# Delta-rule stage of a two-block transformer kernel: heads one by one, and heads in interlocked pairs

## The chip, the cores and the metric

The kernel runs on one core of a Trainium2 chip. The metric is the time on the device in microseconds (us), from the program's start to its end; the number that counts is the median of several executions. One more execution is taken with the hardware profiler; all rows below are from it.

The engines are TensorE (PE; the loading of its weights is shown as PEld), VectorE (DVE), ScalarE (ACT), GpSimd (POOL) and SyncE (SP, which only issues DMAs here). Each runs its own queue in order and waits on semaphores.

## The reference

The whole is a stack of layers on 512 tokens of width 1024: a gated delta rule with attention to a memory of 256 tokens, a gated feed-forward layer, a convolution module, more feed-forward layers and a sparse attention. Only the delta rule changes. For each of 8 heads, with q, k, v from a projection, a causal convolution of four taps and silu:

```python
q = l2norm(q) * GDN_DK ** -0.5
k = l2norm(k)
beta = jax.nn.sigmoid(b)
G = jnp.cumsum(gc, axis=-1)                 # gates
lower = jnp.where(strict, bc[..., :, None] * kk * decay, 0.0)
sol = lax.linalg.triangular_solve(lower + jnp.eye(CHUNK, dtype=f32), rhs, ...)
...
def step(state, xs):                        # over the chunks
    v_new = u_n - jnp.einsum("bhcd,bhde->bhce", w_n, state)
    o_n = jnp.einsum("bhcd,bhde->bhce", qg_n, state) + jnp.einsum("bhij,bhje->bhie", p_n, v_new)
    state = state * gl_n[..., None, None] + jnp.einsum("bhcd,bhce->bhde", kg_n, v_new)
    return state, o_n
...
o = rms_norm(o, out_norm) * jax.nn.silu(split_heads(z, GDN_HEADS).astype(jnp.float32))
```

## The kernel before, in words

Tokens lie along the free axis (512 columns), features along the 128 partitions. The delta rule works in chunks of 128 tokens, so a head has four chunks, and a "product of four" below is one 128x128 matmul for each of them, in fp32, into one PSUM bank of 512 columns.

**Projections.** A weight is split into a high part WR and a low part WL, and a product is three matmuls of 512 columns (lines 281 to 283) per 128 input features. Eight such triples make one unit, one row of 128 features of q, k, v or z of a head. In this text a triple is called a piece. GpSimd makes WR (line 226, a cast) and WL (line 246, a subtraction of 128x1024) of each unit in time; two units are held. `group_chunks` is a generator of pieces of the next head, and `gap(n)` takes n pieces from it, so that they stand among the small products of the current head.

**A head** (`head_tensor`, `head_scalar`, `head_vector`; loop over heads 1 to 6, heads 0 and 7 written out): a sum over partitions makes the gate rows; k and v are turned; k times k gives the lower matrix; T starts as identity less its first level and is turned into U; q times k gives pT. Then six levels of the inverse. Each level is a product of four A = low x U (line 722), ScalarE's copy As (line 852), U's product T x As (line 730), T's product As x T (line 735), and VectorE's subtractions from U (line 931) and T (line 934). Then the recurrence over four chunks: keys x S (745), X on VectorE (949), v = U x X (749), its copy (952), the state sum (759) and the output (760), the state update on VectorE (956, 958). Beside this run the rows of the next head: ScalarE copies a projected row out of its bank (770), VectorE does the four taps (799, 801), ScalarE silu, squares and the roots of the norms. The finished head is normalised, gated and split (884 to 890) while the next one runs.

**Order.** Four units of head 0 come first, then the gates of all heads (`gates_tensor`, `decays_vector`), then the heads. After head 7 comes the attention to the memory, whose q rows are projected among head 7's products. There is one buffer for every tile, and one PSUM bank for each of A, U, T, output and so on.

## Time and profile before

| | us |
|---|---|
| median of 3 executions | 2425.77 (2422.97 to 2431.35) |
| the profiled execution, its own time | 2426.29 |
| its span, first to last instruction | 2424.5 |
| TensorE busy | 2257.6 (93%) |
| VectorE busy | 1204.0 (50%) |
| ScalarE busy | 970.3 (40%) |
| GpSimd busy | 767.1 (32%) |

The delta-rule stage is the part of the span from about 85 to 564 us. Matmuls are pipelined, so the recorded durations overlap: what a matmul costs in a row of others is the distance from its start to the next one's start. A timeline merges like instructions that follow each other into one line, with their count behind an x.

### The profile page before, as it was taken

What the parts mean: (1) busy time and instruction counts of PE and PEld (TensorE: products, weight loads), DVE (VectorE), ACT (ScalarE), POOL (GpSimd) and SP (SyncE); (2) the same over time, 40 slices, a digit from 0 to 9 for tenths busy, and PEclk for the clock granted to TensorE, in tenths of its full rate; (3) what the DMA queues carried; (4) which work ended last, traced back from release to release, by engine and by line L of the source; (5) the groups of instructions that cost most, each with busy time, mean ns of one, the idle gap of its engine ahead of it and who ended that gap; (6) DMA issues with size and microseconds to landing.
All of it is one profiled execution on the core that took longest, in us unless ns stands there. A gap on an engine that the chain in (4) does not pass through costs nothing.

```text
span 2424.5 us, 31521 instructions
## 1 busy us (share of the span) xinstructions
PE 2257.6 (93%) x10534; PEld 1782.7 (74%) x10534; DVE 1204.0 (50%) x1906; ACT 970.3 (40%) x1612; POOL 767.1 (32%) x336
## 2 busy tenths in 40 slices
PE   3799999998989999989979999999999989999997
PEld 2677777776768888858847888888766657888886
DVE  5366666664243332259974333324566764333322
ACT  4434333433343232265544444322455454444322
POOL 2522222221424444410013444444410103444442
PEclk7999999998999999999989999999999999999999
DMA  3210111111322223211102222322100002222322
GB/s 124 97 35 35 38 39 35 35 40 48 104 66 99 96 95 108 92 44 53 52 18 87 97 101 95 124 96 76 61 11 16 17 9 70 99 100 95 101 98 78
DMA packets 43626, 168.83 MB, mean 70 GB/s; under 512 B 4848, under 2 KB 4912, under 8 KB 43056
## 3 DMA queue, kind: packets, MB, share of 16 engines
q1 hardware_dynamic: 43056, 163.82, 19.5%
q10 hardware_dynamic: 512, 4.24, 0.4%
q8 instruction: 35, 0.57, 0.1%
q14 instruction: 23, 0.19, 0.0%
HBM read 165.95 MB, written 2.10 MB: 69 GB/s over the span
## 4 chain that ended last, share of the span: by engine, by line
PE 79%; DVE 9%; issue 5%; ACT 4%; POOL 1%; DMA 1%; DVEq 0%; ACTq 0%; POOLq 0%; SPq 0%
PE bank L281 21%; PE bank L283 21%; PE bank L282 21%; PE bank L1796 2%; PE bank L730 2%; PE bank L722 2%; PE bank L735 1%; DVE act L801 1%; POOL WL L246 1%; ACT Pr L1846 1%; PE bank L1760 1%; PE bank L1778 1%; PE bank L1313 1%; PE bank L1315 1%; PE bank L1314 1%
## 5 line engine op out<-in xcount | busy, mean ns | idle before, releaser
L246 POOL TENSOR_TENSOR WL<-raw,WR 128x1024 fp32r<-128x1024 f32 (+2 forms) x274 | 705.3, 2574 | 1021.9 <-ACT WR L242 1017.2
L281 PE MATMUL bank<-XR,WR 128*128 128x512 f32 x1528 | 631.0, 413 | 30.4 <-DVE XL L426 15.3
L283 PE MATMUL bank<-XR,WL 128*128 128x512 f32 x1528 | 600.3, 393 | 0.0
L282 PE MATMUL bank<-XL,WR 128*128 128x512 f32 x1528 | 599.4, 392 | 0.0
L242 ACT ACTIVATE WR<-raw 128x1024 fp32r<-128x1024 f32 (+2 forms) x230 | 256.2, 1114 | 753.8 <-PE bank L283 746.3
L281 PEld LDWEIGHTS bank<-XR,WR 128*128 128x128 f32 x1528 | 290.1, 190 | 102.9 <-issue 31.9
L281 PE MATMUL bank<-MR,WR 128*128 128x512 f32 (+1 forms) x856 | 336.9, 394 | 16.3 <-DVE ML L1482 7.5
L282 PEld LDWEIGHTS bank<-XL,WR 128*128 128x128 f32 x1528 | 290.3, 190 | 62.7 <-issue 9.9
L283 PEld LDWEIGHTS bank<-XR,WL 128*128 128x128 f32 x1528 | 289.2, 189 | 61.6
L282 PE MATMUL bank<-ML,WR 128*128 128x512 f32 (+1 forms) x856 | 332.9, 389 | 0.0
L283 PE MATMUL bank<-MR,WL 128*128 128x512 f32 (+1 forms) x856 | 332.6, 389 | 0.0
L226 POOL CAST WR<-raw 128x1024 fp32r<-128x1024 f32 (+1 forms) x58 | 61.7, 1064 | 609.7 <-PE bank L283 526.7
L281 PEld LDWEIGHTS bank<-MR,WR 128*128 128x128 f32 x856 | 163.2, 191 | 53.1 <-issue 13.2
L1269 DVE TENSOR_TENSOR f_up<-bank,R 128x512 f32<-128x512 f32 x66 | 45.6, 692 | 302.7 <-PE bank L283 302.7
L283 PEld LDWEIGHTS bank<-MR,WL 128*128 128x128 f32 x856 | 163.3, 191 | 32.9
L282 PEld LDWEIGHTS bank<-ML,WR 128*128 128x128 f32 x856 | 163.5, 191 | 30.6 <-issue 0.2
L402 DVE TENSOR_TENSOR ACC<-ACC,SQ 128x512 f32<-128x512 f32 (+1 forms) x56 | 86.5, 1546 | 144.1 <-ACT SQ L391 142.8
L1274 DVE TENSOR_TENSOR ML<-f_mid,MR 128x512 f32 x66 | 123.1, 1865 | 64.5 <-ACT MR L1252 64.5
L1212 DVE TENSOR_TENSOR hT<-bank,hT 128x512 f32 (+1 forms) x24 | 16.6, 692 | 161.0 <-PE bank L283 161.0
L1846 ACT ACTIVATE Pr<-Pr,stats 128x512 f32<-128x512 f32 (+3 forms) x128 | 70.3, 551 | 58.2 <-DVE stats L1917 58.2
L1267 DVE TENSOR_TENSOR f_gate<-bank,R 128x512 f32<-128x512 f32 x66 | 45.6, 691 | 92.0 <-PE bank L283 71.9
L426 DVE SCALAR_TENSOR_TENSOR XL<-hT,params,XR (+1 forms) x40 | 69.4, 1735 | 33.8 <-ACT XR L422 33.7
(295 smaller groups left out, 2785.9 us busy)
## 6 DMA issues: line engine op xcount, KB each, us to landing
raw<-w SPq DMA_DIRECT2D x224, 512.0 KB, 3.2
raw<-w SPq DMA_DIRECT2D x48, 704.0 KB, 4.1
raw<-w SPq DMA_DIRECT2D x16, 384.0 KB, 3.1
hT<-xT SPq DMA_DIRECT2D x1, 2048.0 KB, 8.1
hT<-xT ACTq DMA_DIRECT2D x1, 2048.0 KB, 8.3
out<-Y SPq DMA_DIRECT2D x8, 256.0 KB, 2.0
memT<-memT ACTq DMA_DIRECT2D x1, 1024.0 KB, 8.1
phi<-phi ACTq DMA_DIRECT2D x1, 1024.0 KB, 6.3
```

The costliest lines, as they stand in the source:

```text
L226: nc.gpsimd.tensor_copy(WR[:, here], raw[:, here]).then_inc(high_split, 1)
L242: nc.scalar.activation(WR[:, here], raw[:, here], ACT.Identity).then_inc(high_ahead, 1)
L246: nc.gpsimd.tensor_tensor(WL[:, here], raw[:, here], WR[:, here].bitcast(F32), ALU.subtract).then_inc(weight_split, 1)
L281: nc.tensor.matmul(into, wr, xr(k0 + k), start=start, stop=False)
L282: nc.tensor.matmul(into, wr, xl(k0 + k), start=False, stop=False)
L283: mm = nc.tensor.matmul(into, wl, xr(k0 + k), start=False, stop=stop)
L402: nc.vector.tensor_tensor(ACC[:, 0:width], ACC[:, 0:width], SQ[:, parity * SEQ:parity * SEQ + width], ALU.add).then_inc(summed, 1)
L426: nc.vector.scalar_tensor_tensor(dst, src, gain, high.bitcast(F32), ALU.mult, ALU.subtract).then_inc(input_ready, 1)
L722: mm = nc.tensor.matmul(bank[4][:, here], joins[:, here], g_["U"][:, here], start=True, stop=True)
L730: mm = nc.tensor.matmul(bank[5][:, here], g_["T"][:, here], g_["As"][:, here], start=True, stop=True)
L1274: nc.vector.tensor_tensor(cols(ML, n), f_mid[:, :], cols(MR, n).bitcast(F32), ALU.subtract).then_inc(mid_low, 1)
L1846: ins = nc.scalar.activation(here, here, ACT.Exp, bias=stat(idx, 0)[:, b:b + 1], scale=-1.0, accum_out=stat(idx, 1)[:, b:b + 1])
```

## The change

Heads are taken in pairs (e = 0, 1), four pairs, all written out. Every tile of a head exists twice, and so does every bank: 2+e, 4+e and 6+e; banks 0 and 1 stay with the projections. The two heads take turns: in each level of the inverse TensorE does A for both, then U for both; in the recurrence each step is done for both before the next.

T is no longer updated by a product and a subtraction. From level 1 on, TensorE turns U (four transposes into bank 6+e), and the result is copied as T: head 0's by ScalarE, head 1's by VectorE.

The projections stand in blocks `gap(4)` to `gap(12)` ahead of the inverse, 48 pieces in all; there are none within the inverse, eleven in the recurrence and the rest behind it. The weights are reordered for this: six units (k, v, q of pair 0) come before the gates; then per pair k and v of the next, z of the present, q of the next; the last pair has z and the memory's q. The gates are copied by VectorE behind all six convolution rows of pair 0. VectorE does three convolution rows of the next pair, and the two query rows of the present one, ahead of the inverse. z goes through silu as it leaves its bank. Queries overwrite their activation, and squares and roots share a tile. Waits are on constants.

The core of the diff, with the new queues of the three engines (removed lines are those of the functions printed above; the copying of rows, the silu, square and root helpers change their tiles and counts only):

```diff
+        def conv_unit(p, kind, e):
+            return 2 * kind + e if p == 0 else 8 * p - 2 + (0, 2, 6)[kind] + e
+        def z_unit(p, e):
+            return (8 * p + 10 if p < PAIRS - 1 else 8 * p + 6) + e
...
+        def pair_tensor_g(pe, p):
+            c, last = p + 1, p == PAIRS - 1
...
+            gap(4)
+            if p:
+                for e in BOTH:
+                    output_norm_tensor(pe, p, e, bank[4 + e])
+            gap(6)
+            for e in BOTH:
+                pe.wait_ge(s_["keys_ready"], nth2(e, c))
+                if p:
+                    pe.wait_ge(s_["o_copied"], nth2(e, p))
+                for b in range(NB):
...
+            gap(8)
+            for e in BOTH:
+                pe.wait_ge(s_["gap_ready"], nth2(e, c))
+                pe.wait_ge(s_["row_decay_ready"], nth2(e, c))
+                norm_tensor(pe, p, 2, e)
+            gap(8)
+            for e in BOTH:
+                pe.wait_ge(s_["T_ready"], nth2(e, c))
+                for b in range(NB):
+                    mm = nc.tensor.transpose(bank[6 + e][:, of_chunk(b)], G("T", e)[:, of_chunk(b)], ident)
+                mm.then_inc(s_["T_turned"], 1)
...
+            gap(12)
+            for e in BOTH:
+                pe.wait_ge(s_["queries_ready"], nth2(e, c))
+                for b in range(NB):
+                    mm = nc.tensor.matmul(bank[2 + e][:, of_chunk(b)], G("keys", e)[:, of_chunk(b)], G("act_q", e)[:, of_chunk(b)],
+                                          start=True, stop=True)
+                mm.then_inc(s_["qk_done"], 1)
+            gap(10)
+            for lv in range(LEVELS - 1):
+                for e in BOTH:
+                    joins = G("low_a" if lv % 2 == 0 else "low_b", e)
+                    pe.wait_ge(s_["low_ready"], nth2(e, 6 * p + lv + 1))
+                    if lv == 0:
+                        pe.wait_ge(s_["U_ready"], nth2(e, c))
+                        pe.wait_ge(s_["pT_ready"], nth2(e, c))
+                    else:
+                        pe.wait_ge(s_["U_moved"], nth2(e, 6 * p + lv))
+                    for b in range(NB):
+                        mm = nc.tensor.matmul(bank[2 + e][:, of_chunk(b)], joins[:, of_chunk(b)], G("U", e)[:, of_chunk(b)], start=True, stop=True)
+                    mm.then_inc(s_["A_done"], 1)
+                    if lv:
+                        for b in range(NB):
+                            mm = nc.tensor.transpose(bank[6 + e][:, of_chunk(b)], G("U", e)[:, of_chunk(b)], ident)
+                        mm.then_inc(s_["T_done"], 1)
+                for e in BOTH:
+                    pe.wait_ge(s_["A_ready"], nth2(e, 6 * p + lv + 1))
+                    if lv:
+                        pe.wait_ge(s_["T_moved"][e], 5 * p + lv)
+                    else:
+                        pe.wait_ge(s_["k_gained_ready"], nth2(e, c))
+                    for b in range(NB):
+                        mm = nc.tensor.matmul(bank[4 + e][:, of_chunk(b)], G("T", e)[:, of_chunk(b)], As[e][:, of_chunk(b)], start=True, stop=True)
+                    mm.then_inc(s_["U_done"], 1)
+            gap(2)
+            for e in BOTH:
+                pe.wait_ge(s_["U_moved"], nth2(e, 6 * p + 6))
+                pe.wait_ge(s_["q_decayed_ready"], nth2(e, c))
             for b in range(NB):
...
+                here = of_chunk(b)
+                if b:
+                    for e in BOTH:
+                        pe.wait_ge(s_["S_ready"], nth2(e, 3 * p + b))
+                        nc.tensor.matmul(bank[4 + e][:, 0:P], G("keys", e)[:, here], G("S", e), start=True, stop=True).then_inc(s_["kS_done"], 1)
+                    gap(1)
+                for e in BOTH:
+                    if b:
+                        pe.wait_ge(s_["X_ready"], nth2(e, 3 * p + b))
+                    rhs = G("X", e) if b else G("v_beta", e)[:, here]
+                    nc.tensor.matmul(bank[4 + e][:, P:2 * P], G("U", e)[:, here], rhs, start=True, stop=True).then_inc(s_["v_done"], 1)
+                    if b:
+                        nc.tensor.matmul(bank[6 + e][:, here], G("S", e), G("q_decayed", e)[:, here], start=True, stop=False)
+                if b == 1 and not last:
+                    for e in BOTH:
+                        norm_tensor(pe, p + 1, 0, e)
+                gap(2)
+                for e in BOTH:
+                    pe.wait_ge(s_["v_ready"], nth2(e, 4 * p + b + 1))
+                    if b < NB - 1:
+                        nc.tensor.matmul(bank[4 + e][:, 2 * P:3 * P], G("k_gained", e)[:, here], G("v_new", e), start=True, stop=True).then_inc(s_["S_sum_done"], 1)
+                    mm = nc.tensor.matmul(bank[6 + e][:, here], G("v_new", e), G("pT", e)[:, here], start=b == 0, stop=True)
+                    if b == NB - 1:
+                        mm.then_inc(s_["o_done"], 1)
+            gap(64)
...
+                for e in BOTH:
+                    act.wait_ge(s_["A_done"], nth2(e, 6 * p + lv + 1))
+                    nc.scalar.activation(As[e], bank[2 + e][:, :], ACT.Identity).then_inc(s_["A_ready"], 1)
+                    if lv and e == 0:
+                        act.wait_ge(s_["T_done"], nth2(e, 5 * p + lv))
+                        nc.scalar.activation(G("T", e), bank[6 + e][:, :], ACT.Identity).then_inc(s_["T_moved"][e], 1)
...
+        def pair_vector_g(dve, order, p):
+            V = nc.vector
+            c, last = p + 1, p == PAIRS - 1
+            for e in BOTH:
+                dve.wait_ge(s_["rows_done"], nth2(e, c))
+                order.link(V.tensor_tensor(blocks(G("D_E", e)), blocks(bank[2 + e][:, :]), over_columns(row4(cum, 2 * p + e)), ALU.subtract))
+                V.scalar_tensor_tensor(G("D_E", e), G("D_E", e), -1.0, G("D_E", e), ALU.mult, ALU.max).then_inc(s_["gap_ready"], 1)
+            if p:
+                for e in BOTH:
+                    whole(conv_steps(dve, p, 2, e))
+                output_vector(dve, order, p)
+            for e in BOTH:
+                m = G("lower", e)
+                dve.wait_ge(s_["kk_done"], nth2(e, c))
+                dve.wait_ge(s_["decay_ready"], nth2(e, c))
+                order.link(V.tensor_tensor(m, bank[6 + e][:, :], G("D_E", e), ALU.mult))
+                order.link(V.tensor_tensor(blocks(m), blocks(m), over_columns(row4(beta, 2 * p + e)), ALU.mult))
+                order.link(V.tensor_tensor(blocks(G("low_b", e)), blocks(m), over_blocks(const(LEVEL0)), ALU.mult))
+                V.tensor_tensor(blocks(G("T", e)), over_blocks(ident), blocks(G("low_b", e)), ALU.subtract).then_inc(s_["T_ready"], 1)
+                V.tensor_tensor(blocks(G("low_a", e)), blocks(m), over_blocks(const(LEVEL0 + 1)), ALU.mult).then_inc(s_["low_ready"], 1)
+            for e in BOTH:
+                dve.wait_ge(s_["v_turned"], nth2(e, c))
+                V.tensor_tensor(blocks(G("v_beta", e)), blocks(bank[4 + e][:, :]), over_columns(row4(beta, 2 * p + e)), ALU.mult).then_inc(s_["v_beta_ready"], 1)
+            if p:
+                output_low_vector(dve, p)
+            if not last:
+                whole(conv_steps(dve, p + 1, 0, 0))
+            for e in BOTH:
+                dve.wait_ge(s_["norms_rooted"], nth2(e, 2 * p + 2))
+                V.scalar_tensor_tensor(G("act_q", e), G("act_q", e), QS, G("norm", e), ALU.mult, ALU.mult).then_inc(s_["queries_ready"], 1)
...
+            if not last:
+                whole(conv_steps(dve, p + 1, 0, 1))
+            for e in BOTH:
+                dve.wait_ge(s_["k_turned"], nth2(e, c))
+                V.tensor_tensor(blocks(G("k_gained", e)), blocks(bank[4 + e][:, :]), over_columns(row4(k_gain, 2 * p + e)), ALU.mult).then_inc(s_["k_gained_ready"], 1)
+                dve.wait_ge(s_["T_ready"], nth2(e, c))
+                V.tensor_tensor(blocks(G("low_b", e)), blocks(G("lower", e)), over_blocks(const(LEVEL0 + 2)), ALU.mult).then_inc(s_["low_ready"], 1)
+            if not last:
+                whole(conv_steps(dve, p + 1, 1, 0))
+            for e in BOTH:
+                dve.wait_ge(s_["qk_done"], nth2(e, c))
+                order.link(V.tensor_tensor(G("pT", e), bank[2 + e][:, :], G("D_E", e), ALU.mult))
+                V.tensor_tensor(blocks(G("pT", e)), blocks(G("pT", e)), over_blocks(tri), ALU.mult).then_inc(s_["pT_ready"], 1)
...
+                if lv:
+                    dve.wait_ge(s_["T_done"], nth2(1, 5 * p + lv))
+                    V.tensor_copy(G("T", 1), bank[7][:, :]).then_inc(s_["T_moved"][1], 1)
+                for e in BOTH:
+                    dve.wait_ge(s_["U_done"], nth2(e, 6 * p + lv + 1))
+                    V.tensor_tensor(G("U", e), G("U", e), bank[4 + e][:, :], ALU.subtract).then_inc(s_["U_moved"], 1)
+                if lv < LEVELS - 3:
+                    for e in BOTH:
+                        low = G("low_a" if lv % 2 == 0 else "low_b", e)
+                        V.tensor_tensor(blocks(low), blocks(G("lower", e)), over_blocks(const(LEVEL0 + lv + 3)), ALU.mult).then_inc(s_["low_ready"], 1)
```

## Rows read from the trace of the kernel before

**Rows 1.** Table of stretches, one head of the loop: length, busy time (count), clock, DMA share.
```profile
231.00:287.00 56.00, 51.91 (x304) 41.19 (x302) 37.94 (x57) 22.94 (x35) 13.84 (x9) 1.00 0.11 37
```

**Rows 2.** Timeline, all engines, one level of the inverse: start, length, engine, line, operation.
```profile
247.95 1.05 PE L722 MATMUL bank<-U,low_b 128*128 128x128 f32 x8
...
249.04 0.60 ACT L852 ACTIVATE As<-bank 128x512 f32<-128x512 f32 x1 [4.42 <-PE bank L722]
...
249.77 1.15 PE L730 MATMUL bank<-As,T 128*128 128x128 f32 x8
...
250.76 1.06 PE L735 MATMUL bank<-T,As 128*128 128x128 f32 x8
250.96 0.69 DVE L931 TENSOR_TENSOR U<-U,bank 128x512 f32<-128x512 f32 x1 [0.20 <-PE bank L730]
...
251.57 0.48 PE L281 MATMUL bank<-XR,WR 128*128 128x512 f32 x1
...
253.05 1.05 PE L722 MATMUL bank<-U,low_a 128*128 128x128 f32 x8
```

**Rows 3.** Timeline, TensorE, the recurrence and the start of the next head.
```profile
273.71 0.46 PE L749 MATMUL bank<-v_beta,U 128*128 128x128 f32 x2 [0.93 <-DVE U L931]
...
275.98 0.49 PE L759 MATMUL bank<-v_new,k_gained 128*128 128x128 f32 x2 [1.11 <-DVE v_new L952]
...
276.85 0.49 PE L745 MATMUL bank<-S,keys 128*128 128x128 f32 x2 [0.16 <-DVE S L956]
...
277.96 0.49 PE L749 MATMUL bank<-X,U 128*128 128x128 f32 x2
...
281.01 0.49 PE L745 MATMUL bank<-S,keys 128*128 128x128 f32 x2 [0.33 <-DVE S L958]
...
287.61 1.12 PE L679 MATMUL bank<-D_E,table 128*128 128x512 f32 x2
288.56 0.60 PE L683 MATMUL bank<-table,act 128*128 128x128 f32 x4
```

**Rows 4.** Timeline, TensorE, first piece of head 0's 32 and what follows the last.
```profile
85.43 0.47 PE L281 MATMUL bank<-XR,WR 128*128 128x512 f32 x1 [1.50 <-POOL WL L246]
...
107.40 0.44 PE L617 MATMUL bank<-table,gates 40*128 40x40 f32 x4
```

**Rows 5.** Timeline, TensorE, four transposes and the piece behind them.
```profile
240.21 0.60 PE L700 MATMUL bank<-table,T 128*128 128x128 f32 x4
240.56 0.48 PE L281 MATMUL bank<-XR,WR 128*128 128x512 f32 x1
```

**Rows 6.** Timeline, VectorE and GpSimd; last, a group of lines from 231 to 455.
```profile
102.70 1.05 DVE L799 TENSOR_SCALAR act<-pre,params 128x512 f32<-128x512 f32 x1
103.79 4.34 DVE L801 SCALAR_TENSOR_TENSOR act<-pre,params,act 128x512 f32<-128x512 f32 x3
...
269.78 2.43 POOL L246 TENSOR_TENSOR WL<-raw,WR 128x1024 fp32r<-128x1024 f32 x1
...
270.12 2.63 DVE L801 SCALAR_TENSOR_TENSOR act<-pre,params,act 128x512 f32<-128x512 f32 x1
...
L914 DVE TENSOR_TENSOR lower<-lower,scalars 128x512 f32<-128x512 f32 x4 | 2.8, 692 | 0.1
```

**Rows 7.** Table of stretches, the inverse of one head and a part of a recurrence.
```profile
243.70:272.60 28.90, 28.46 (x185) 23.90 (x183) 22.33 (x29) 8.89 (x14) 8.36 (x5) 1.00 0.10 36
331.00:334.00 3.00, 2.18 (x8) 1.83 (x9) 1.14 (x4) 2.54 (x3) 0.00 (x0) 0.66 0.00 1
```

**Rows 8.** Timeline, VectorE's first copy of the gates, TensorE's first transposes of v.
```profile
108.16 0.19 DVE L603 COPY scalars<-bank 128x32 f32<-128x32 f32 x1
...
120.59 1.12 PE L683 MATMUL bank<-table,act 128*128 128x128 f32 x4 [2.44 <-ACT r_q L826]
```

**Rows 9.** Timeline, TensorE, last chunk of the recurrence of head 7.
```profile
561.21 0.49 PE L745 MATMUL bank<-S,keys 128*128 128x128 f32 x2 [0.22 <-DVE S L958]
562.21 0.49 PE L749 MATMUL bank<-X,U 128*128 128x128 f32 x2 [0.51 <-DVE X L949]
...
563.08 0.49 PE L760 MATMUL bank<-pT,v_new 128*128 128x128 f32 x2 [0.16 <-DVE v_new L952]
```

More of the change, by code:

```diff
@@ L662, in query_norm_tensor, with unit_bank @@
[L662 to L672 removed]
+        def unit_bank(u):
+            return bank[(seg_g.tile0 + u) % 2]
```

605 lines of the change are left out of this document (282 added, 323 removed).

## The prediction

> **What bounds the kernel now.** I began with the table of stretches. In one head of the loop, TensorE is busy 51.9 of 56.0 us and VectorE 37.9; ScalarE and GpSimd are far below [rows 1]. So the stage of the delta rule hangs on TensorE, with VectorE the next limit at two thirds. The timeline says what TensorE's 56 us are made of. A level of the inverse starts every 5.10 us (247.95 to 253.05) [rows 2]: product A 0.81 (the same four products as T's, 250.76 to 251.57), a piece of projection, then product U, which does not start before 1.82 us after A, because ScalarE's copy starts 1.09 after A and lasts 0.60. U takes 0.99, since its first weights are loaded only after the wait, T 0.81, and two pieces of projection 1.48. Of the 5.10 some 0.4 is stall. After the last level the recurrence runs to 287.6, 15 us [rows 3], with nine pieces' worth of work: five pieces of projection (0.75 each), 17 small products (0.22) and two sums over partitions (0.9). That is 9.3 of 15. The reader is to see the holes: 275.98 to 276.85 for one state update, 276.85 to 277.96 for X. Together a head has about 47.5 us of work and 8.4 of stall.
>
> **Prices.** A piece of projection (three matmuls) is 0.687, from 32 pieces between 85.43 and 107.40 [rows 4]; one that follows other work costs 0.085 more (its first matmul 0.31 and not 0.23 before the next; in a head, two pieces behind a product take 1.48 [rows 2] where 2 x 0.687 is 1.37). Four 128x128 products: 0.81 [rows 2]. Four transposes: 0.35 (240.21 to 240.56) [rows 5]. A sum over partitions of 512 columns: 0.95 (287.61 to 288.56) [rows 3]; I take 0.85 to 0.95.
>
> **The change on TensorE.** (1) T is no longer computed by a product but by transposing U: five times per head 0.81 becomes 0.35, 2.3 us per head, 18 in all. (2) The projections stand in blocks of 4 to 12 pieces: 14 changes from fp32 work to projection in a pair instead of some 44, so 2.5 us per pair. (3) The holes are filled with the other head.
>
> Per pair, in the order of the new queue. Before the inverse: two row sums 1.9, 48 pieces in six blocks 33.5, two output norms and two query norms 3.4, key and query products 3.4, three sets of transposes 2.1: 44.4. The inverse, level 0: A0 A1 U0 U1, with the waits of [rows 2] (copy 1.8 behind A, U's subtraction 1.2 behind U and 0.69 long): 3.7. Levels 1 to 5: A0, turn 0, A1, turn 1 are 2.3 us, then U0 and U1. U0 needs As0 and T0 from ScalarE, ready at 2.4 to 2.5; U1 needs T1 from VectorE, turned at 2.5, seen at 2.8, copied at 3.5, so it starts at 3.5 instead of 3.3 and pays 0.18 for its weights. The next A0 needs U0's subtraction, ready at 4.3, and TensorE is free at 4.5. I take 4.45 per level, against 3.96 of pure work: 22.3, the inverse 26.0. The recurrence: two heads' small products 7.5, eleven pieces inside with their changes 8.6, two key norms 1.8, last pieces 2.1, plus what stays open at four state updates (0.2 each) and behind the last U: 22.4. One pair is 92.8, where two heads took 111.7.
>
> **What VectorE does to that.** Its work moves. Before the inverse of a middle pair it has 32 operations of 512 columns at 0.61 to 0.73 apart (0.69 long [rows 6]) and five convolution rows. A row not disturbed is one scalar and three fused operations: 4.34 for three, with one of them stretched to 2.63, leaves 0.85 each [rows 6], so 3.1 per row. 21 + 15.5 + 1.3 before the first row sum: 38 us, below 44.4. But an operation of VectorE with two operands in SBUF that starts inside GpSimd's low-part subtraction ends 0.5 after it: 270.12, 2.63 long, against 269.78, 2.43 long [rows 6]. In the old order such a pass often fell on pauses of VectorE and on its reads of PSUM. In the new one VectorE hardly rests, and six subtractions of 2.4 lie in the stretch (one per unit of eight pieces), each costing some 2.0 to 2.2: +13. By a walk of both queues pT of head 0 is ready at 51.1 us, and the first A of the inverse waits for it, since it overwrites the bank that pT reads. TensorE would be there at 44.5: a wait of 6.7. Queued behind the waiting product is the whole inverse; ScalarE waits with it. Behind such a hole I add 2 for products at the lower clock [rows 7]. So pairs 1 and 2: 92.8 + 6.7 + 2 = 101.5. Pair 0 has no query rows and no output to finish (VectorE's end 38 us, TensorE's 42.8), pair 3 has no next rows: no wait. Pair 0: 91.2.
>
> **The two ends.** Six units instead of four go first: 33.0 us, to 118.4. Six rows of convolution at 5.4 (1.05 and 4.34 [rows 6]) keep VectorE until 124.7; only then does it copy the gates, which it did at 108.16. From there the transposes of v stood 12.4 us off (120.59) [rows 8]; silu and squares, about 4.4 of these, are by now done, though the row sums now wait for the roots. I take 8 (bounds 6 and 12.4): pair 0 starts at 132.5. Pair 3 has 48 pieces, all ahead of its inverse, none to fill its recurrence: 44.4 + 26.0, then steps of 1.0 (X) and 0.87 (v) [rows 9] and 0.87 (S) [rows 3], the second head nearly in their shade: 11.5, plus 1.5 for a fallen clock: 83.5. Then two heads' roots and outputs instead of one: +3 before the memory attention goes on. All four pairs are straight-line code. The old head 7 is too, and its X took 1.00 [rows 9] where the loop took 1.11 [rows 3]. So waits on constants gain at most 0.1 each, some 4 us over 40 such steps, and fetching the longer code costs nothing that these rows show; I take 0 for both, the 4 us stand in the range.
>
> **The sum.** 132.5 + 91.2 + 2 x 101.5 + 83.5 = 510.2 for the end of the last output, which is 563.6 now (563.08 and the 0.49 of its products) [rows 9]: 53.4 less. With +3: 50.4 less. The profiled execution took 2426.3 us around its span of 2424.5; the median of the runs is 2425.8, the same for this purpose. 2426.3 - 50.4 = 2375.9; I say 2375.
>
> [...] In the recurrence of the next head the granted clock of three microseconds is 0.66, after TensorE had idled twice for about a microsecond, and products there slow down [rows 7]. The new inverse has no projection in it, small waits, and a third of its instructions of a level are transposes. [...]
>
> **The rivals.**
> A. VectorE's collisions cost little (GpSimd's pass falls on PSUM reads or waits): no hole in pairs 1 and 2. 2375.9 - 17.4 = 2358. For it: in the old head four passes cost only some 4.5 us. Against: there VectorE had pauses.
> B. The turns don't interlock: each level costs both heads' chains one after the other, 5.10 less two pieces and T, twice: 5.6 instead of 4.45. 20 levels x 1.15 = +23: 2399. For it: U0 and U1 each hang on two engines. Against: all waits I walked come to under 0.3 per level.
> [...]
> D. The pairs don't close up: VectorE, which has to serve both heads' chains and the next rows, sets the pace in pairs 1 and 2, and they take what two heads take now. The price is 2 x (111.7 - 101.5) = +20: 2396. For it: the new stretch before the inverse is full on VectorE. Against: the walk leaves it 40 us of light work in the inverse and the recurrence.
>
> **Chances.** Forecast 0.50 (its own range 2362 to 2390), A 0.20, B 0.13, D 0.06, C 0.06, more gain than A 0.05. The range takes in A, B, D and the bounds of the start (-2, +4): 2348 to 2400. A measurement of this kernel tells about 0.3%, 7 us, from no change. Faster by more 0.92, within 0.03 (C with a short fall of the clock), slower 0.05.
>
> **What would show it.** Right: levels 4.3 to 4.6 apart per pair; no L735-like product; the first A of pairs 1 and 2 released by pT, 5 to 8 us late; VectorE's fused operations of 2 to 2.6 us in step with GpSimd; clock 1.00 in the inverse; pair 0 starting near 132. Wrong if the granted clock in the inverse is near 0.5, if pairs are longer than 105, or if the pieces after the delta rule have moved in length.

## The result, and the profile after

The changed kernel takes 2401.74 us (median of 4 executions, 2398.77 to 2404.09) against 2428.28 before (median of 4 on the same chips, 2422.97 to 2431.35): a ratio of 0.9892, with a 95% interval from 0.9871 to 0.9912. The profiled execution took 2398.77 us around a span of 2396.8. The forecast was 2375, its range 2348 to 2400: about half of the gain came, and the median lies 1.7 us outside the range.

The timeline of TensorE in the changed kernel, at the places of which the sum speaks (start, length, engine, line, operation, out<-in, how many, and in brackets the idle time before it with what ended it). L709 is the row sum that opens a pair, L744 the transposes of the keys, L764 product A, L768 the transposes of U, L777 product U, L805 the outputs:

```profile
133.12 3.75 PE L709 MATMUL bank<-D_E,table 128*128 128x512 f32 x4 [2.81 <-ACT norm L854]
180.13 1.13 PE L764 MATMUL bank<-U,low_a 128*128 128x128 f32 x8 [1.90 <-DVE pT L1026]
182.89 0.98 PE L764 MATMUL bank<-U,low_a 128*128 128x128 f32 x3 [1.63 <-DVE pT L1026]
192.04 1.06 PE L764 MATMUL bank<-U,low_a 128*128 128x128 f32 x8
192.94 0.60 PE L768 MATMUL bank<-table,U 128*128 128x128 f32 x4
193.38 1.06 PE L764 MATMUL bank<-U,low_a 128*128 128x128 f32 x8
194.27 0.60 PE L768 MATMUL bank<-table,U 128*128 128x128 f32 x4
194.71 2.17 PE L777 MATMUL bank<-SQ,T 128*128 128x128 f32 x16
196.71 0.50 PE L764 MATMUL bank<-U,low_b 128*128 128x128 f32 x3
...
231.77 1.45 PE L709 MATMUL bank<-D_E,table 128*128 128x512 f32 x3
261.50 1.76 PE L744 MATMUL bank<-table,keys 128*128 128x128 f32 x7 [2.70 <-DVE v_beta L1002]
285.50 1.40 PE L764 MATMUL bank<-U,low_a 128*128 128x128 f32 x5 [4.77 <-DVE pT L1026]
335.17 1.02 PE L709 MATMUL bank<-D_E,table 128*128 128x512 f32 x2
388.92 1.41 PE L764 MATMUL bank<-U,low_a 128*128 128x128 f32 x5 [5.97 <-DVE pT L1026]
439.74 1.02 PE L709 MATMUL bank<-D_E,table 128*128 128x512 f32 x2
522.92 0.81 PE L805 MATMUL bank<-pT,v_new 128*128 128x128 f32 x4
557.97 0.79 PE L281 MATMUL bank<-MR,WR 128*128 128x512 f32 x1
```

The pairs start at 133.12, 231.77, 335.17 and 439.74, so they last 98.65, 103.4 and 104.6 us, and the last runs 83.2 us to the start of its last outputs. The levels are 4.67 apart (192.04 to 196.71), where one head's level took 5.10 [rows 2]. The first piece of out1, the projection after this stage, starts at 557.97. In the kernel before it is this row:

```profile
597.06 0.79 PE L281 MATMUL bank<-MR,WR 128*128 128x512 f32 x1
```

So the delta rule gave 39.1 us, and the profiled executions differ by only 27.5 at the end. Whatever else is missing was lost after the changed code. The sums of squares that close the stages (L408) show where. These are the ones ahead of and behind the second block's attention, first before, then after:

```profile
1676.66 1.02 PE L408 MATMUL bank<-ACC,table 128*128 128x512 f32 x2
2051.30 1.02 PE L408 MATMUL bank<-ACC,table 128*128 128x512 f32 x2
```

```profile
1636.71 1.02 PE L408 MATMUL bank<-ACC,table 128*128 128x512 f32 x2
2023.53 1.02 PE L408 MATMUL bank<-ACC,table 128*128 128x512 f32 x2
```

From 374.64 us the stretch has grown to 386.82, by 12.2, though no line of it was changed. VectorE's loop in it has three passes, one for each turn but the last. The second and third, counted from the branch that closes the one before, take 73.25 and 73.27 us where they took 68.76 and 67.79: 10.0 of the 12.2. VectorE's timeline at the first return of its loop over the turns of the attention shows this, with TensorE's first operation behind it:

```profile
1767.40 0.69 DVE L2066 TENSOR_TENSOR ML<-bank,MR 128x512 f32 x1 [2.48 <-ACT MR L1967]
1770.43 0.18 DVE L2043 RECIPROCAL stats<-stats 128x4 f32<-128x4 f32 x1 [2.34 <-issue]
1773.01 0.17 DVE L2048 TENSOR_TENSOR stats<-stats,gates 128x4 f32<-128x4 f32 x1 [2.41 <-issue]
...
1774.54 2.40 PE L1882 MATMUL bank<-table,Pr 128*128 128x128 f32 x10 [4.63 <-DVE Pr L2058]
```

L2066 ends the body of the loop, L2043 begins it. "issue" means that nothing the profile records held VectorE up, twice, for 2.34 and 2.41 us. TensorE waited 4.63 us for the result. The same pair of gaps stands at the second return (2.42 before 1843.75, 2.22 before 1846.15). The same place in the kernel before has none:

```profile
1806.48 0.69 DVE L1962 TENSOR_TENSOR ML<-bank,MR 128x512 f32 x1 [2.47 <-ACT MR L1863]
1807.09 0.17 DVE L1939 RECIPROCAL stats<-stats 128x4 f32<-128x4 f32 x1
1807.41 0.17 DVE L1944 TENSOR_TENSOR stats<-stats,gates 128x4 f32<-128x4 f32 x1 [0.16 <-DVE stats L1939]
```

The DMA view of the 20 us around the second return names the transfers that ran meanwhile. The only queue in it is one for instructions (packets, MB, share of the engines), 4 packets of 8 KB, and its packets move where VectorE stands: at the first return they start at 1768.5 and 1771.2 us, 0.4 and 0.6 us into the two gaps, at the second at 1841.9 and 1844.3, 0.5 and 0.3 us into them. So it is taken to be VectorE's:

```profile
q14 instruction: 4, 0.03, 0.6%
```

Over the whole program it has 36 packets after and 23 before. In the stretch with both returns (1755 to 1940 us, before 1795 to 1943) it has 11 after and none before.

The table of stretches (length; busy time with counts of TensorE, its weight loads, VectorE, ScalarE, GpSimd; granted clock; DMA) shows what the gaps cost besides their length, in the stretches around the two returns. Before, the corresponding 20 us (1796:1816, the first return) have TensorE busy for 19.67 with the clock at 1.00:

```profile
1764.00:1784.00 20.00, 15.37 (x56) 9.78 (x56) 7.94 (x31) 7.53 (x23) 2.54 (x2) 0.74 0.00 2
1836.00:1856.00 20.00, 15.50 (x59) 10.19 (x59) 9.15 (x35) 7.60 (x23) 1.42 (x2) 0.74 0.01 2
```

### The profile page after: what moved, and what is told of

Same layout as the page of the kernel before. It is cut to its first block, busy times and chain, and to the rows that moved or that the text cites. A ratio compares the mean times of both kernels' runs of the same rounds, so it can differ in the third digit from the quotient of the medians.

```text
span 2396.8 us, 30556 instructions
## 1 busy us (share of the span) xinstructions
PE 2228.1 (93%) x10374; PEld 1777.9 (74%) x10374; DVE 1217.8 (51%) x1886; ACT 970.4 (40%) x1621; POOL 777.4 (32%) x336
## 4 chain that ended last, share of the span: by engine, by line
PE 75%; DVE 13%; issue 7%; ACT 4%; POOL 1%; DMA 1%; DVEq 0%; ACTq 0%; POOLq 0%; SPq 0%
PE bank L281 20%; PE bank L282 20%; PE bank L283 19%; PE bank L1900 2%; PE bank L777 2%; PE bank L764 2%; POOL WL L246 1%; PE bank L1882 1%; ACT Pr L1950 1%; DVE act_q L954 1%; DVE act_v L954 1%; PE bank L1419 1%; PE bank L1418 1%; PE bank L1417 1%; PE bank L768 1%
## 5 line engine op out<-in xcount | busy, mean ns | idle before, releaser
L281 PE MATMUL bank<-XR,WR 128*128 128x512 f32 x1528 | 619.3, 405 | 29.9 <-DVE XL L426 15.0
```

Source lines behind the costliest of these rows:

```text
L281: nc.tensor.matmul(into, wr, xr(k0 + k), start=start, stop=False)
```

## The experiments

Two questions: what stalls VectorE in a loop that was not touched (theory F, its code has to be fetched again, because the longer straight-line code ahead of it moved it), and what makes the pairs longer than their work. Except where it says otherwise, each kernel is the changed one with the loop head of e1, so e1 (2394.57 us) is what it is compared with. Stages that an edit doesn't touch differ between executions: from out1 to the sum ahead of the attention these kernels take 1076 or 1079 us without any pattern, and the last turn of the attention, straight-line code behind the loop, takes 59.7 to 66.5 us. So the stretch of the attention takes 374.6 to 380.2 us in the kernels without a gap at the returns, and 386.8 to 389.0 in the three that have them.

### Where the loop stands

e1 puts the loop's first instruction at slot 47, counted in 256 (in e1 and e2 the loop's body is the same, apart from the hint):

```diff
-            with dve.Fori(0, TURNS - 1) as i:
+            with nc.Fori(0, TURNS - 1, engines=OrderedEngineSet([dve.engine]), head_slot={dve.engine: 47}) as i:
```

> The changed kernel with one thing moved: the head of VectorE's loop over the turns of the second attention (three iterations of some 70 us, the loop in attend_vector) is loaded at instruction slot 47 of a fetch block, which is about where the kernel before has it by a count of its instructions; the padding is branched over. Theory F (code fetching): the four stalls of 2.2 to 2.4 us at the back edges of this loop (at 1770, 1773, 1844 and 1846 us of the changed kernel's trace) are the loop body's instructions being fetched again, because the longer delta rule moved the body across one more block; with the head moved the stalls are gone, the instruction queue carries fewer packets between 1764 and 1856 us, and the end comes 9 to 12 us earlier: 2390 to 2393 where the changed kernel has 2401.7, a ratio to before of 0.984 to 0.986. Rival N (chance of the run, or weights arriving late in the attention): nothing but the padding changes, the stalls stay, and the time stays at 2400 to 2403.

Measured: 2394.57 us (2392.17 to 2396.29), ratio 0.9871 (0.9855 to 0.9888). The four gaps at the returns are gone, and the two passes take 66.87 and 66.92 us. One gap of 2.84 stands where the loop is entered, right behind the branch over the padding (e3 and e4 have such a branch and no gap there, so the branch alone isn't its cause). The instruction queue has 28 packets, none of them between 1764 and 1856 us, where the changed kernel has 9. The loss was theory F's, with 7 of the 9 to 12 us back; the stretch is at 380.20 and not at 374.64, since the last turn took 66.5 us here and 60.0 before.

e2 leaves the loop where it is and announces the branch at the top of the body:

```diff
+            with nc.Fori(0, TURNS - 1, engines=OrderedEngineSet([dve.engine]), hint_back_edge=True) as i:
```

> The changed kernel, its loop head left where it is, with a hint ahead of the body of the same VectorE loop that names the target of the branch that closes it. 
Measured: 2391.62 us (2390.11 to 2392.37), ratio 0.986 (0.9844 to 0.9877). No gap is left at either return, and the instruction queue has 26 packets, none of them between 1755 and 1940 us; so the narrow form would do. One gap of 1.29 stands in the last turn, at 1947.57. The hint hasn't moved the head: the three hints inside the body are all that VectorE's queue has more in the trace. The stretch of the attention is 374.64 us again; that it agrees to the hundredth with before is chance, given how the last turn varies:

```profile
1639.87 1.02 PE L409 MATMUL bank<-ACC,table 128*128 128x512 f32 x2
...
2014.51 1.02 PE L409 MATMUL bank<-ACC,table 128*128 128x512 f32 x2
```

The other way round, three kernels take the old delta rule and move only the loop. e3:

```diff
+            with nc.Fori(0, TURNS - 1, engines=OrderedEngineSet([dve.engine]), head_slot={dve.engine: 239}) as i:
```

> The kernel before, with nothing of the change, and the head of the same VectorE loop loaded at slot 239 of a fetch block. Theory F: the placement alone brings the stalls: two back edges with one or two stalls of 2.2 to 2.4 us each at the loop's return and the weights' matmuls after them at a lower clock, so 5 to 12 us more than before: 2433 to 2440, ratio 1.002 to 1.005. Rival N (the loss in the attention belongs to the changed delta rule by another way, such as the weights' buffers): the time is that of before, 2428, within 0.1%.

Measured: 2427.21 us against 2425.72, ratio 1.0004 (0.9994 to 1.0014), no gap at the returns, 23 packets (its stretch of the attention takes 379.94 us all the same, 71.7 of them in one pass without any gap). A miss: either F is wrong or 239 is the wrong slot. e9 and e10 decide it with a better count (this is e9; e10 has offset=232):

```diff
+            dve.addr_align(256, offset=104, max_nops=0)
+            for _ in range(20):
+                dve.sem_inc(passed, 1)
             with dve.Fori(0, TURNS - 1) as i:
```

> The kernel before with the head of VectorE's second attention loop near slot 125 of a fetch block: the code is aligned to slot 104 right ahead of the loop and 20 semaphore instructions follow. A head at slot 239 brought no stall, so the count of slots by which 239 was chosen was wrong. The packets of the changed kernel give a better one: its loop fetches 8 KB (128 instructions) about each 32 us of its 73 us, which makes the body some 280 instructions; a stall at the head and a second one two instructions later put its head in the last few slots of such a block, so that the body touches four blocks. Theory F: with the head near slot 125 each of the two back edges has two stalls of 2.2 to 2.4 us, as in the changed kernel, some 9 to 12 us more than before, 2434 to 2438. [...] Rival N (the delta rule's change reaches the attention in another way): neither this kernel nor the next stalls.

> The same with the head near slot 253 of 256: aligned to slot 232, 20 semaphore instructions after it. Theory F with 8 KB blocks: the same stalls as with 125. [...] Rival N: 2426 to 2428 in both.

Measured: e9 2439.08 us (2438.0 to 2441.84), ratio 1.0052 (1.0036 to 1.0069); e10 2443.84 us (2439.06 to 2444.79), ratio 1.0064 (1.0045 to 1.0082), against 2425.9 for before. Both have two gaps at each return (in e10 of 2.55, 2.04, 2.29 and 1.81 us) and one at the entry, 34 and 33 packets. At the returns one packet starts within 0.45 us of the start of every gap (in e9 at 1805.6, 1808.0, 1878.9 and 1881.3). The first return in e9:

```profile
1807.50 0.18 DVE L1940 RECIPROCAL stats<-stats 128x4 f32<-128x4 f32 x1 [2.31 <-issue]
1807.84 0.17 DVE L1945 TENSOR_TENSOR stats<-stats,gates 128x4 f32<-128x4 f32 x1 [0.16 <-DVE stats L1940]
1809.80 1.27 DVE L1955 TENSOR_SCALAR Pr<-Pr,stats 128x512 f32<-128x512 f32 x4 [1.79 <-issue]
```

The old delta rule with nothing moved but this loop (and 20 semaphore instructions and the padding ahead of it) is slower by 13 and 18 us, and its stretch of the attention takes 388.95 and 388.67 us. That settles theory F: the place of the loop brings the gaps, and with them a loss of the size of the 12 us, of which some 2 are within what the stretch varies by. It also tells the size that counts. A packet is 8 KB, and between two fetches within one pass (1805.8 and 1838.1 us in the changed kernel) the trace records 130 instructions of VectorE's queue. Heads near 125 and near 253 are alike, so blocks of 128 count; a head at 239, which is slot 111 of such a block, is harmless. A body that fits three blocks from slot 111 and touches four from slot 125 has between 260 and 273 instructions (worked out from these runs), and the trace records 264 in each pass. So without the hint a body that touches four blocks has two packets fetched at each return while VectorE stands, at 1.8 to 2.6 us a gap (changed kernel, e9, e10), and one that fits three has none: e1 has no packet between 1764 and 1856 us.

### What makes the pairs long

e4 undoes the turning of U: T comes from a product and a subtraction, as before.

```diff
-                    if lv:
-                        for b in range(NB):
-                            mm = nc.tensor.transpose(bank[6 + e][:, of_chunk(b)], G("U", e)[:, of_chunk(b)], ident)
...
+                    if lv < LEVELS - 2:
+                        for b in range(NB):
+                            mm = nc.tensor.matmul(bank[6 + e][:, of_chunk(b)], As[e][:, of_chunk(b)], G("T", e)[:, of_chunk(b)], start=True, stop=True)
...
+                        V.tensor_tensor(G("T", e), G("T", e), bank[6 + e][:, :], ALU.subtract).then_inc(s_["T_moved"][e], 1)
```

> The changed kernel with the loop head at slot 47 and with one part of the change undone: T comes from the product of As and T and a subtraction on VectorE, as before, in place of transposes of U copied by ScalarE and VectorE. Theory (the inverse is bound by TensorE, and four transposes take 0.35 us where four products take 0.81): 40 products in place of 40 transposes cost 0.46 us each, 18.4 us, so 2408 to 2412 with the first delta rule's levels 5.6 us apart in place of 4.67. Rival 1 (the levels are bound by the turn-around between engines, not by TensorE): levels under 5.0 apart, and less than 8 us lost. [...]

Measured: 2403.34 us (2397.24 to 2411.1), ratio 0.9908 (0.9879 to 0.9937). From the first pair's start to the last output it takes 404.7 us where e1 takes 390.3, so 14.4 more, and out1 starts 13.6 later (574.68, 561.1). By the medians it is 8.8 us above e1 and short of the 2408 to 2412 expected: its executions spread over 14 us, and the profiled one has 2.5 back in the stretch of the attention (377.69, 380.20). The levels are 5.42 apart:

```profile
303.93 1.95 PE L765 MATMUL bank<-U,low_a 128*128 128x128 f32 x16
305.72 1.11 PE L774 MATMUL bank<-SQ,T 128*128 128x128 f32 x8
306.67 1.06 PE L778 MATMUL bank<-T,SQ 128*128 128x128 f32 x8
307.56 1.06 PE L774 MATMUL bank<-SQ,T 128*128 128x128 f32 x8
308.46 1.06 PE L778 MATMUL bank<-T,SQ 128*128 128x128 f32 x8
309.35 0.83 PE L765 MATMUL bank<-U,low_b 128*128 128x128 f32 x6
```

Six sets of four products at 0.90 fill these 5.42 us without a hole. With transposes the level has four such sets and two turns of 0.44 (192.94 to 193.38), 4.48 us, and lasts 4.67. So turning saves 2 x 0.46 of work, and 0.2 of it is given back as a wait at product U: 0.75 per level, 15 us in 20. Rival 1, levels under 5.0, is out. Both kernels have the clock at 1.00 there (303.93:320.19 and 192:206), so the transposes don't lower it.

e5 moves one row of convolution from ahead of pT into the levels:

```diff
-            if not last:
-                whole(conv_steps(dve, p + 1, 1, 0))
             for e in BOTH:
                 dve.wait_ge(s_["qk_done"], nth2(e, c))
...
+            early = iter(()) if last else conv_steps(dve, p + 1, 1, 0)
             for lv in range(LEVELS - 1):
...
+                if lv:
+                    next(early, None)
```

> The changed kernel with the loop head at slot 47 and one VectorE row moved: the convolution of the next pair's first value row (4 operations, 5.6 us in the trace, disturbed by GpSimd) goes from ahead of pT into levels 1 to 4 of the inverse, one operation after each level's masks, where VectorE is idle 0.8 us and GpSimd has nothing to do. Theory (the waits for pT are VectorE's queue being too long before the inverse): the waits of TensorE for pT in pairs 1 and 2 (4.77 and 5.97 us) go, those of pair 0 (3.5) too, and the clock after them holds: 12 to 17 us less than with the loop head alone. Rival (the operations in the levels delay the subtractions, TensorE being full there): the levels grow from 4.67 to over 5.0 us, which takes back 4 to 6 us of it.

Measured: 2377.12 us (2370.15 to 2380.71), ratio 0.9804 (0.9788 to 0.9821), 17 less than e1. The pairs last 93.6, 98.3, 98.6 and 83.2, the levels 4.67 as before, and what is left of the waits for pT is 0.59 in pair 1. The wait for v_beta (2.69 and 2.70) still stands in pairs 1 and 2. The rival, longer levels, is out.

e6 puts the transposes of the keys later:

```diff
                 mm.then_inc(s_["T_turned"], 1)
+            gap(6)
             for e in BOTH:
                 pe.wait_ge(s_["v_beta_ready"], nth2(e, c))
...
                 mm.then_inc(s_["k_turned"], 1)
-            gap(12)
+            gap(6)
```

> The changed kernel with the loop head at slot 47 and the eight transposes of the keys (which wait for v_beta) put six pieces later on TensorE, in the middle of the twelve pieces that follow them. Theory (v_beta is late by 2.7 us in pairs 1 and 2, and six pieces of 0.69 us cover it): these waits go; pT is bound by VectorE, not by TensorE, so the time comes back as a longer wait for pT, and only 0 to 2 us are gained. Rival (each wait costs its own length and a lower clock after it): 5 to 8 us gained.

Measured: 2394.15 us (2387.91 to 2396.88), ratio 0.9863 (0.9845 to 0.988): nothing gained, as the theory had it; the rival is out. The wait for v_beta is gone and stands in the next ones: in pair 1 TensorE waits 1.60 us for act_q and then 7.30 for pT, where the changed kernel had 2.70 and 4.77 and e1 2.70, 2.23 and 0.72:

```profile
287.98 0.55 PE L766 MATMUL bank<-U,low_a 128*128 128x128 f32 x1 [7.30 <-DVE pT L1028]
```

e7 gives the start another order (the two halves of gates_tensor have four pieces between them, the first pair's query rows follow its row sums, and ScalarE's steps move along):

```diff
-            for _ in unit_chunks(pe, 0, 6):
-                pass
-            gates_tensor(pe)
...
+            gap(8)
+            gates_tensor(pe, gap)
+            gap(28)
             for e in BOTH:
                 norm_tensor(pe, 0, 0, e)
+            gap(64)
...
-            for kind in range(3):
+            decays = decays_vector(dve, order)
+            next(decays, None)
+            for kind in range(2):
                 for e in BOTH:
                     whole(conv_steps(dve, 0, kind, e))
-            decays_vector(dve, order)
+                    next(decays, None)
```

> The changed kernel with the loop head at slot 47 and the start of the delta rule put in another order: the gates are turned and summed after the first projection unit instead of the sixth, the key norms' roots are taken ahead of the last rows' silu, and the two query rows of the first pair are convolved inside the pair, as in later pairs, instead of ahead of it. Theory (the 14.5 us between the last projection piece at 118.6 us and the pair's start at 133.1 are VectorE's queue and not the data): pair 0 starts at 119 to 122 us, takes 101 to 105 us in place of 98.7, since it now has the other pairs' VectorE work, and 7 to 10 us are gained. Rival (VectorE's total work sets the time of the inverse of pair 0): the pair takes 110 us and no more than 3 us are gained.

Measured: 2380.53 us (2371.77 to 2381.94), ratio 0.9801 (0.9781 to 0.9822), 14 less than e1. Pair 0 starts at 124.21 and not at 134.84, right behind the last piece, and lasts 98.9, no longer than before. These 10.6 us are the edit's; the other 3.5 fell in the stages between out1 and the attention, which it doesn't touch. So the start was VectorE's queue, the theory's place, though neither of its two numbers.

e8 leaves out the subtraction that makes the low part of the delta rule's weights; GpSimd copies the loaded weights in its place, so its projections are not the reference's:

```diff
+            if seg is SEG["gdn"]:
+                wait_apart(pool, high_split, unit + (seg.own0 - seg.unit0 + 1))
+                nc.gpsimd.tensor_copy(WL[:, here], raw[:, here]).then_inc(weight_split, 1)
+                return
             pool.wait_ge(high_split, unit + (seg.own0 - seg.unit0 + 1))
             low_unit(seg, slot)
```

> The changed kernel with the loop head at slot 47, in which GpSimd makes the low part of the delta rule's weights by a copy of the loaded weights in place of the subtraction of the high part (the subtraction is left out, so the projections are not the reference's). Theory (GpSimd's two-input operations lengthen VectorE's two-input operations to 2.6 to 2.9 us, and that is what makes pT late): the VectorE operations beside them take 1.2 to 1.4 us, the waits for pT and v_beta in pairs 1 and 2 go, and 12 to 20 us are gained. Rival (VectorE's own work is too long there anyway): the operations get shorter, the waits stay over half of what they were, and less than 7 us are gained.

Measured: 2359.31 us (2354.72 to 2360.51), ratio 0.972 (0.9704 to 0.9737), 35 less than e1: 30.0 in the four pairs, 2.8 ahead of them, and the rest mostly between out1 and the attention, which the edit doesn't touch. No wait for pT or v_beta is left, and the pairs last 93.3, 92.6, 92.6 and 81.8. VectorE and GpSimd at the start of pair 1, first in e8, then in the changed kernel:

```profile
227.20 1.34 DVE L991 SCALAR_TENSOR_TENSOR D_E<-D_E 128x512 f32<-128x512 f32 x1
229.17 0.69 DVE L991 SCALAR_TENSOR_TENSOR D_E<-D_E 128x512 f32<-128x512 f32 x1
...
226.95 1.04 POOL L230 CAST WL<-raw 128x1024 fp32r<-128x1024 f32 x1 [0.17 <-POOL WR L227]
```

```profile
233.55 2.62 DVE L986 SCALAR_TENSOR_TENSOR D_E<-D_E 128x512 f32<-128x512 f32 x1
236.81 0.69 DVE L986 SCALAR_TENSOR_TENSOR D_E<-D_E 128x512 f32<-128x512 f32 x1
...
233.22 2.40 POOL L246 TENSOR_TENSOR WL<-raw,WR 128x1024 fp32r<-128x1024 f32 x1
```

The same operation takes 0.69 alone, 1.34 against a copy of 1.04 and 2.62 against a subtraction of 2.40, and both times it ends 0.55 us behind GpSimd's: it waits until that is over. GpSimd isn't late itself: in e1 TensorE waits 1.4 us for it in the whole stage.

The gain was twice what was expected, since only the waits were priced. Pair 1 came out 11.1 shorter (103.7 in e1, 92.6) though its waits in e1 are 2.70 + 2.23 + 0.72, 5.65 us. The rest is slower products behind each wait: up to the wait for v_beta the changed kernel's pair 1 and that of e8 run alike to 0.02 us, and the twelve pieces between the keys' transposes and the product of keys and queries, with these transposes, take 10.5 us behind the wait and 9.1 without it (granted clock 0.86 in 261.50:272.00, and 1.00 in e8). Level 0 of pair 1 takes 5.21 us in the changed kernel (285.50 to 290.71) and 3.86 where it doesn't wait. The granted clock stands last but two in each line:

```profile
192.00:206.00 14.00, 14.00 (x122) 13.57 (x122) 9.80 (x15) 5.05 (x9) 0.00 (x0) 1.00 0.01 2
285.50:291.00 5.50, 5.48 (x34) 5.32 (x35) 3.30 (x6) 1.19 (x2) 0.00 (x0) 0.75 0.31 95
388.00:396.00 8.00, 7.00 (x38) 6.87 (x39) 4.69 (x9) 1.19 (x2) 0.00 (x0) 0.62 0.21 66
```

### Together

e11 is the changed kernel with the edits of e2, e5, e6 and e7.

> The changed kernel with the four mends together: the hint for the loop's back edge (2391.6 measured alone), the first value row's convolution in the levels (17 us less than with the loop head alone), the gates early (14 us less), and the transposes of the keys six pieces later, which was worth nothing while pT was late and should now be worth the two waits of 2.70 us and the lower clock after them. Theory (the causes add up, since each wait that was hidden behind pT is gone too): 2391.6 - 17 - 14 - 6, so 2352 to 2360. Rival (pT becomes late again, because pair 0 now has the other pairs' VectorE work and the keys' transposes no longer give slack): 2362 to 2372.

Measured: 2365.28 us (2362.19 to 2369.61), ratio 0.974 (0.9726 to 0.9754). The rival came: the pairs last 93.3, 101.3, 100.3 and 82.4, and pT is late again, by 1.92 and 1.64. Pair 1 waits 1.60 us for act_q and 3.56 for pT, where e5 waits 2.69 for v_beta and 0.59 for pT: 1.9 more with one more wait mended. e12 takes more off VectorE's queue:

```diff
-            for e in BOTH:
-                dve.wait_ge(s_["row_decay_ready"], nth2(e, c))
-                dve.wait_ge(s_["queries_ready"], nth2(e, c))
-                V.tensor_tensor(G("q_decayed", e), G("q_decayed", e), G("act_q", e), ALU.mult).then_inc(s_["q_decayed_ready"], 1)
...
+                if lv >= LEVELS - 3:
+                    e = lv - (LEVELS - 3)
+                    dve.wait_ge(s_["row_decay_ready"], nth2(e, c))
+                    dve.wait_ge(s_["queries_ready"], nth2(e, c))
+                    V.tensor_tensor(G("q_decayed", e), G("q_decayed", e), G("act_q", e), ALU.mult).then_inc(s_["q_decayed_ready"], 1)
```

> The kernel with the four mends, with three things moved: the two products q_decayed (2.4 us of VectorE ahead of pT) go into the last two levels, where VectorE has 2.0 us free; the first value row's four operations start with level 0 instead of 1; and the keys' transposes come after 5 of the pieces, the product of keys and queries after 9 more, with 8 left. In the trace before it TensorE waits 1.6 us for act_q and 1.92 and 1.64 us for pT in each of pairs 1 and 2, with the clock lower after them; these pairs take 101.3 and 100.3 us. Theory (VectorE's queue ahead of pT is what is late, by less than 2.4 us now): the waits shrink under 1 us each, pairs 1 and 2 take 93 to 96 us (92.6 where GpSimd's subtraction was left out), and the time is 2349 to 2357. Rival (what VectorE gets rid of comes back, since an operation that ends earlier meets the next of GpSimd's subtractions and is lengthened by it): the pairs keep 99 us or more, 2360 to 2366.

Measured: 2364.55 us (2363.06 to 2364.7), ratio 0.9736 (0.9715 to 0.9757): no change against e11. The rival came: pairs 1 and 2 take 100.7 and 100.0, and TensorE waits 4.65 us for pT in each. VectorE has 2.4 us less to do ahead of pT, and pT of head 0, for which the first product A waits, is ready later. First e11, then e12, each with GpSimd's subtraction:

```profile
262.98 0.81 DVE L1029 TENSOR_TENSOR pT<-pT,table 128x512 f32<-128x512 f32 x1
264.42 2.13 DVE L1029 TENSOR_TENSOR pT<-pT,table 128x512 f32<-128x512 f32 x1
...
263.32 2.68 POOL L247 TENSOR_TENSOR WL<-raw,WR 128x1024 fp32r<-128x1024 f32 x1
```

```profile
262.88 2.12 DVE L1025 TENSOR_TENSOR pT<-pT,table 128x512 f32<-128x512 f32 x1
265.63 0.69 DVE L1025 TENSOR_TENSOR pT<-pT,table 128x512 f32<-128x512 f32 x1
...
261.78 2.67 POOL L247 TENSOR_TENSOR WL<-raw,WR 128x1024 fp32r<-128x1024 f32 x1
```

It ends at 265.00 and not at 263.79. The rows ahead of it met other subtractions as well: the convolution of the second key row took 5.6 us (1.25 and 4.34) where it took 3.5 in e11. So the lateness of pT follows not from the sum of VectorE's work alone but from where the subtractions fall in it. Which order would dodge them all stays open; it wasn't tried. e11 and e12 beat the changed kernel by 36 and 37 us and the one before by 61 and 62.

## Why the prediction was wrong, step by step

**Fetching, the step that failed most.** "Fetching the longer code costs nothing that these rows show; I take 0" was read off the straight-line code of head 7. In the straight-line pairs that held: VectorE has no gap ended by "issue" between 85 and 560 us. The price fell on a loop 1200 us later whose place the longer code had moved. The stretch around it is 12.2 us longer in the profile, 10.0 of them in the two passes that begin with the gaps, and the cause is shown from both sides (e2 takes the gaps away, e9 and e10 bring them to the old kernel). The prediction named the sign for it, pieces after the delta rule moved in length, and had no price for it in sum or range. Without this loss the kernel takes 2391.62 us (e2), inside the range; so the second step is needed for the miss as well.

**VectorE's queue in pair 0, 91.2 forecast, 98.65 measured.** "No wait" was wrong. VectorE's work ahead of pT was to end 38 us into the pair; pT of head 0 is ready at 179.98, 46.9 us into it; in e8, where GpSimd doesn't subtract, 38.9 us into it. So the subtractions lengthen this work too, and the prediction had added them in pairs 1 and 2 only. pT was late by 1.90 and 1.63, level 0 took 7.18 us (the second of these waits in it) instead of 3.86, and the pair's first ten pieces took 8.3 us, where 10 x 0.69 is 6.9. With the row moved (e5) the pair takes 93.6.

**Pairs 1 and 2, 101.5 forecast, 103.4 and 104.6 measured.** The sum of the work was right: 92.8 forecast, 92.6 where nothing waits (e8). Part of that is luck: the stretch before the inverse takes 44.2 (44.4), the inverse 27.3 (26.0) and the recurrence 21.1 (22.4). The place of the hole was right too, pT of head 0, with 4.77 and 5.97 against 6.7. The wait for v_beta (2.70) was not in the walk; e6 shows that it is only the first part of the same lateness. Under-sized was the clock: the 2 us behind the hole were 3.3 in pair 1 (10.8 longer than its 92.6, of which 7.47 are waits), and 3.3 in pair 2. The collisions were under-sized: VectorE's operations ahead of pT in pair 1 are together some 18 us longer than their shortest copies (an estimate from the trace), where the walk had 13. It lengthened only operations with two operands in SBUF (pT's first one, which reads a bank, took 0.69 at 243.13 in the kernel before, inside a subtraction from 242.80 to 245.17), and the trace has one with a single tensor operand that took 2.62 us instead of 0.47, in the value row ahead of pT (276.97, L951), beside a subtraction from 276.58 to 279.30.

**The inverse.** A level takes 4.67, not 4.45, and two errors partly cancel in that. Its work is 4.48, not 3.96, since four products come to 0.90 and four turns to 0.44 where 0.81 and 0.35 were taken; what stays open is 0.19, not 0.49. These prices were read between single groups and not from the repeat of the pattern. That U's first weights are loaded only behind its wait is in the trace of the kernel before: the load starts at 249.76, after 0.50 us without one, and the product at 249.77. Turning instead of a product was priced at 18 and is worth 14.4 (e4).

**What was right.** Pair 0 starts at 133.12 (132.5), by the causes named: VectorE copies the gates at 125.33 (124.7), and the pair starts 7.8 us later (8). e7 shows that it was VectorE's queue. Pair 3 takes 84.0 to the end of its last outputs (83.5). The clock in the inverse is 1.00 (192:206), where 8 of a level's 24 instructions are transposes, so C, a fallen clock there, is out. B is out by the levels. D would have needed what two heads took before, 112.8 us (231.77 to 344.60; the prediction's 111.7 is twice the shorter of the two). A's mechanism doesn't hold, since the collisions cost 30 us (390.3 in e1, 360.2 in e8, from pair 0 to the last outputs), more than the 17.4 it would have given back.

**The account.** To the end of the last output: 523.7 for 510.2, of which start 0.6, pair 0 7.4, pairs 1 and 2 5.0, pair 3 0.5. From there to out1 the stage takes 0.8 more than before, not 3: 2.2 back. The attention: 12.2. Together 23.5, and the profiled execution is 22.9 above the 2375.9 of the sum. The median is 3 above the profiled execution, which is no more than the executions differ by (2398.77 to 2404.09).

## What to carry to other kernels

Code that gets longer ahead of a long loop moves the loop. Count the body in blocks of 128 instructions (four of them cost two gaps of 1.8 to 2.6 us at each return, three none), pin its head or announce its branch, and compare the stages behind the edit, not only the edited one. When an operation of VectorE meets one of GpSimd, the price is what is left of GpSimd's (0.69 us became 2.62 beside a subtraction of 2.40), and a hole in TensorE costs its length and the slower products behind it (5.65 us of waits cost 11.1 in pair 1 of e1); work saved in such a queue may come back as the next meeting. Price a wait by the stretch that repeats, and try an edit that removes a wait together with what is late next.

## What was not expected of the hardware

- A loop of VectorE that touches four blocks of 128 instructions and not three has two gaps of 1.8 to 2.6 us at each return (changed kernel, e9, e10), and a pass takes 73 to 75 us where it takes 66 to 72 without them; a hint at the top of its body takes the gaps away (e2).
- GpSimd's copies with one input, too, hold up VectorE's operations with two operands in SBUF, from 0.69 to 1.34 us against a copy of 1.04 (e8).
- An operation of VectorE with one tensor operand is held up too: TENSOR_SCALAR took 2.62 us and not 0.47 beside a subtraction (changed kernel, 276.97).
